# The first norm's gain: one row spread by TensorE in place of a broadcast load

## The reference, cut to what matters

```python
def rmsnorm(x, g, eps=NORM_EPS):
    xf = x.astype(jnp.float32)
    y = xf * lax.rsqrt(jnp.mean(xf * xf, axis=-1, keepdims=True) + eps)
    return (y * g.astype(jnp.float32)).astype(x.dtype)
...
        xn = rmsnorm(x, norm_mix_pre[l])
        q, k, v, u_a, v_a = project(xn, w_in[l])
```

## Time and profile before

| | |
|---|---|
| time before, median of 3 runs | 1381.57 us (1380.36 to 1382.99) |
| the profiled execution's own time | 1382.37 us |
| its span | 1380.6 us |
| PE busy in the span | 1357.9 us (98%) |
| DVE, ACT, POOL busy | 701.5, 461.0, 169.9 us |
| granted clock in the page's 40 slices | 9 in each |
| PE busy from 0 to 5 us, 5 to 10, 10 to 15, 15 to 20 | 0.00, 4.34, 3.71, 4.31 us |
| PE busy from 20 to 25, 25 to 30, 30 to 35 us | 5.00, 5.00, 4.88 us |

### The profile page before, as it was taken

How to read it: one execution, slowest core, us unless ns; L and a number is a source line. 1 busy time by engine, 2 the same in 40 slices (tenths; PEclk the granted TensorE clock), 3 DMA queues, 4 the chain that set the end, 5 groups by cost and what they waited for, 6 DMA issues and landing times.

```text
span 1380.6 us, 22412 instructions
## 1 busy us (share of the span) xinstructions
PE 1357.9 (98%) x8658; PEld 1220.7 (88%) x8658; DVE 701.5 (51%) x1173; ACT 461.0 (33%) x782; POOL 169.9 (12%) x323
## 2 busy tenths in 40 slices
PE   7999999999999999999999999999999999999998
PEld 6999999966657788899898989898989898999986
DVE  6233322176778564554546464636454545364556
ACT  6321021055667543343131313131323232222332
POOL 2253000022222221120000000000000000000003
PEclk9999999999999999999999999999999999999999
DMA  7202123266673623132020201111110202010116
GB/s 266 63 31 66 31 77 99 73 193 185 182 234 133 206 103 119 47 107 77 16 76 15 75 17 61 30 61 30 58 33 22 69 15 76 15 64 27 47 46 134
DMA packets 93577, 113.17 MB, mean 82 GB/s; under 512 B 6460, under 2 KB 65509, under 8 KB 93509
## 3 DMA queue, kind: packets, MB, share of 16 engines
q1 hardware_dynamic: 90377, 105.26, 24.2%
q0 software_dynamic: 992, 3.54, 1.5%
q10 hardware_dynamic: 2140, 3.46, 0.7%
HBM read 97.28 MB, written 14.69 MB: 81 GB/s over the span
## 4 chain that ended last, share of the span: by engine, by line
PE 93%; DVE 2%; issue 2%; ACT 1%; DMA 1%; POOL 0%; SPq 0%; POOLq 0%; DVEq 0%; ACTq 0%
PE PS L2361 37%; PE PS L2073 17%; PE PS L2425 16%; PE PS L2304 7%; PE PS L2166 2%; PE PS L2128 2%; PE PS L2189 2%; PE PS L2440 2%; PE PS L2455 2%; PE PS L2235 1%; PE PS L2212 1%; PE PS L2058 1%; DMA x_in<-in_x_prompt_dram 1%; PE PS L2296 1%; PE PS L2154 1%
## 5 line engine op out<-in xcount | busy, mean ns | idle before, releaser
L2361 PE MATMUL PS<-act_lo,wu_hi 128*128 128x364 f32 (+1 forms) x1056 | 346.4, 328 | 0.0
L2361 PE MATMUL PS<-act_hi,wu_hi 128*128 128x364 f32 (+1 forms) x1056 | 346.0, 328 | 0.2 <-DVE wu_lo L1850 0.2
L2361 PE MATMUL PS<-act_hi,wu_lo 128*128 128x364 f32 (+1 forms) x1056 | 346.0, 328 | 0.0
L2361 PEld LDWEIGHTS PS<-act_hi,wu_hi 128*128 128x128 f32 x1056 | 198.6, 188 | 1.0 <-DVE wu_lo L1850 0.5
L2361 PEld LDWEIGHTS PS<-act_lo,wu_hi 128*128 128x128 f32 x1056 | 198.2, 188 | 0.4
L2361 PEld LDWEIGHTS PS<-act_hi,wu_lo 128*128 128x128 f32 x1056 | 198.4, 188 | 0.0
L1836 DVE TENSOR_TENSOR y_acc<-y_acc,PS 128x512 f32<-128x512 f32 x162 | 111.1, 686 | 116.0 <-PE PS L2425 116.0
L2425 PE MATMUL PS<-wd_hi,g_hi 128*128 128x512 f32 x324 | 130.1, 401 | 0.0
L2425 PE MATMUL PS<-wd_lo,g_hi 128*128 128x512 f32 x324 | 127.9, 395 | 0.0
L2425 PE MATMUL PS<-wd_hi,g_lo 128*128 128x512 f32 x288 | 114.0, 396 | 0.0
L1230 ACT CAST g_hi<-conv 128x1088 fp32r<-128x1088 f32 x21 | 23.1, 1102 | 245.6 <-PE PS L2425 189.6
(11 more groups left out here) (280 smaller groups left out, 2382.7 us busy)
## 6 DMA issues: line engine op xcount, KB each, us to landing
wu_raw<-in_w_up_dram SPq DMA_DIRECT2D x44, 512.0 KB, 3.9
vpage<-in_cache_v_dram SPq DMA_DIRECT2D x64, 256.0 KB, 3.0
kpage<-in_cache_k_dram SPq DMA_DIRECT2D x60, 256.0 KB, 2.9
wd_raw<-in_w_down_dram SPq DMA_DIRECT2D x22, 512.0 KB, 5.3
w_raw<-in_w_in_dram SPq DMA_DIRECT2D x20, 512.0 KB, 4.7
x_in<-in_x_prompt_dram SPq DMA_DIRECT2D x8, 512.0 KB, 7.0
wo_raw<-in_w_out_dram SPq DMA_DIRECT2D x8, 512.0 KB, 5.6
x_res<-in_x_prompt_dram SPq DMA_DIRECT2D x8, 512.0 KB, 4.2
```

Source lines behind the costliest of these rows:

```text
L2361: mm = nc.tensor.matmul(PS[:, 3 * half + c, 0:kept(c)], a[:, half, k, :], b[:, k, KEPT[c]], start=(j == 0), stop=(j == len(parts) - 1))
```

## The change

The table's broadcast load behind tile 0 goes. In its place DVE zeroes `gain`, ACT's queue loads the 1024 values into its first row, and PE multiplies a 128x128 block of ones (`rel_rep` of head 3, before its own values are written) with it: two matmuls, 512 columns each, which leave the row in all 128 partitions of PSUM banks 2 and 3. Tiles 0 and 1 take the gain from there, and the later tiles from the table in SBUF, which SP now loads behind tile 2, once the two matmuls are done. The bias lines are spread differently over the streams. The rounding of the second weight piece on ACT moves ahead of the squares of tile 1.

```diff
--- before.py
+++ after.py
@@ -739,11 +739,12 @@
                 sp.wait_ge(nrm_ready, s - 2)
             sp.dma_start(x_in[0:rows(s), s % 3, :], x_tiles[s]).then_inc(x_loaded[s % 3], 16)
             if s == 0:
-                sp.dma_start(gain[:], norm_mix_pre[0:1, :].to_broadcast([P, D])).then_inc(gain_loaded, 16)
                 load_w(sp, 0)
             if s == 1:
                 load_w(sp, 1)
             if s == 2:
+                sp.wait_ge(line_ready, 1)
+                sp.dma_start(gain[:], norm_mix_pre[0:1, :].to_broadcast([P, D])).then_inc(gain_loaded, 16)
                 for i, lam in enumerate((lambda_q1, lambda_q2, lambda_k1, lambda_k2)):
                     sp.dma_start(lam_in[:, i, :], lam[0:1, :].to_broadcast([P, DH])).then_inc(setup_loaded, 16)
                 sp.dma_start(sub_gain[:], subln_gain[0:1, :].to_broadcast([P, DV])).then_inc(setup_loaded, 16)
@@ -930,6 +931,8 @@
         act.dma_start(rel_sb[:], rel_bias[:, :]).then_inc(line_loaded, 16)
         act.wait_ge(lines_zero, 1)
         act.dma_start(lines_sb[0:BUCKETS + 1, :], lines[:, :]).then_inc(line_loaded, 16)
+        act.wait_ge(rep_ready, 1)
+        act.dma_start(gain[0:1, :], norm_mix_pre[0:1, :]).then_inc(gain_loaded, 16)
         act.wait_ge(const_ready, 3)
         nc.scalar.activation(stat[:, 104:105], neg_half, ACT.Square)
         for s in range(STEPS):
@@ -943,7 +946,6 @@
             if s == 0:
                 act_split_w(act, 0, (0,))
                 xt_hi(0)
-            if s == 1:
                 act_split_w(act, 0, (1,))
             if s >= 3:
                 take_job(s - 3)
@@ -1432,11 +1434,15 @@
     def _(dve):
         def bias_tables():
 
+            nc.vector.memset(gain[:], 0.0).then_inc(rep_ready, 1)
             nc.vector.memset(rel_rep[:], 1.0).then_inc(rep_ready, 1)
             dve.wait_ge(line_loaded, 16 * 2)
-            dve.wait_ge(rep_ready, 1)
-            for h in range(H):
-                nc.vector.tensor_copy(rel_rep[0:BUCKETS, h, :], rel_sb[:, h:h + 1].to_broadcast([BUCKETS, P])).then_inc(rep_ready, 1)
+            dve.wait_ge(rep_ready, 2)
+            for h in range(H - 1):
+                rep_line(h)
+
+        def rep_line(h):
+            nc.vector.tensor_copy(rel_rep[0:BUCKETS, h, :], rel_sb[:, h:h + 1].to_broadcast([BUCKETS, P])).then_inc(rep_ready, 1)
 
         def lam_tables():
             dve.wait_ge(setup_loaded, 16 * 5)
@@ -1448,7 +1454,7 @@
 
         def take_line(h):
 
-            dve.wait_ge(line_ready, h + 1)
+            dve.wait_ge(line_ready, h + 2)
             nc.vector.tensor_scalar(line_out[:, h, :], PS[:, 4 + h, 0:LINE], -1.0, None, ALU.mult).then_inc(line_taken, 1)
 
         def xt_lo(s):
@@ -1459,29 +1465,31 @@
                                         act_hi[:, 4 * h:4 * h + 4, cols(s)].bitcast(F32),
                                         ALU.subtract).then_inc(xt_lo_ready, 1)
         bias_tables()
-        dve.wait_ge(gain_loaded, 16)
+        take_line(0)
         for s in range(STEPS):
             r = rows(s)
             dve.wait_ge(rstd_ready, s + 1)
+            gained = PS[:, 2:4, :].rearrange("p a b -> p (a b)") if s < 2 else gain
+            if s == 2:
+                dve.wait_ge(gain_loaded, 32)
             if s >= 2:
                 dve.wait_ge(xt_ready, 2 * (s - 1))
             if s == 0:
-                nc.vector.scalar_tensor_tensor(x_nrm[:, 0, 0:512], x_in[:, 0, 0:512], rstd[:, 0:1], gain[:, 0:512],
+                nc.vector.scalar_tensor_tensor(x_nrm[:, 0, 0:512], x_in[:, 0, 0:512], rstd[:, 0:1], gained[:, 0:512],
                                                ALU.mult, ALU.mult).then_inc(half_ready, 1)
             cs = slice(512 if s == 0 else 0, D)
             nc.vector.scalar_tensor_tensor(x_nrm[0:r, s % 2, cs], x_in[0:r, s % 3, cs], rstd[0:r, s:s + 1],
-                                           gain[0:r, cs], ALU.mult, ALU.mult).then_inc(nrm_ready, 1)
+                                           gained[0:r, cs], ALU.mult, ALU.mult).then_inc(nrm_ready, 1)
             if s >= 2:
                 xt_lo(s - 1)
             if s == 0:
-                take_line(0)
-                take_line(1)
+                rep_line(H - 1)
                 dve_split_w(dve, 0, (0,))
                 xt_lo(0)
                 dve_split_w(dve, 0, (1,))
-            if s == 1:
+                take_line(1)
+            if s == 2:
                 take_line(2)
-            if s == 2:
                 take_line(3)
                 lam_tables()
             if s == 8:
@@ -1768,7 +1776,7 @@
         take_rows(NB // 2 - 1)
         split_rest(2)
 
-        dve.wait_ge(gain_loaded, 48)
+        dve.wait_ge(gain_loaded, 64)
 
         def x2_lo(t):
             for h in range(2):
@@ -1944,7 +1952,7 @@
         last_wd(1)
         last_lo(2)
 
-        dve.wait_ge(gain_loaded, 64)
+        dve.wait_ge(gain_loaded, 80)
 
         def last_add(t, half):
             s, n = LAST_TILES[t], 2 * t + half
@@ -2031,7 +2039,7 @@
         def bias_lines(heads):
             pe.wait_ge(line_loaded, 16 * 2)
             for h in heads:
-                pe.wait_ge(rep_ready, h + 2)
+                pe.wait_ge(rep_ready, h + 3)
                 nc.tensor.matmul(PS[:, 4 + h, 0:LINE], rel_rep[:, h, :], lines_sb[:], start=True, stop=True).then_inc(line_ready, 1)
 
         def project(n):
@@ -2074,8 +2082,13 @@
             mm.then_inc(job_ready, 1)
 
 
+        pe.wait_ge(rep_ready, 2)
+        pe.wait_ge(gain_loaded, 16)
+        for half in range(2):
+            mm = nc.tensor.matmul(PS[:, 2 + half, :], rel_rep[:, H - 1, :], gain[:, 512 * half:512 * half + 512], start=True, stop=True)
+        mm.then_inc(line_ready, 1)
         pe.wait_ge(pad_zero, 2)
-        bias_lines((0, 1))
+        bias_lines((0,))
         for s in range(STEPS):
             for h in range(2):
                 j = 2 * s + h
@@ -2091,10 +2104,10 @@
                                              ident[0:rows(s), 0:rows(s)])
                 mm.then_inc(xt_ready, 1)
             if s == 0:
-                bias_lines((2,))
+                bias_lines((1,))
                 pe.wait_ge(xt_lo_ready, 1)
                 project(0)
-                bias_lines((3,))
+                bias_lines((2, 3))
             if s >= 2:
                 pe.wait_ge(xt_lo_ready, 2 * s)
                 project(s - 1)
```

## The result

The change makes the kernel slower: 1386.22 us (median of 8 runs, 1384.7 to 1386.98) against 1381.55 (8 runs, 1380.21 to 1386.42), ratio 1.0031 with a 95% interval of 1.0022 to 1.0040. The forecast was 1384.3, range 1382.7 to 1386.3. The profiled execution took 1386.07 us with a span of 1384.3, against 1382.37 and 1380.6: 3.7 us more.

A forecast was written before the change was run, and what follows sets the result against it. PE is the bound, through the start of project(1) at 18.95 us. The change's steps put it at 21.65, 2.7 us late: 1385.1 against the profiled 1382.37, 1384.3 as a median, range 1382.7 to 1386.3.

The forecast's parts named there:

- gain matmuls start (T): On PE, 0.15 us after the row lands: 5.55 us, between 4.25 and 6.15; later steps are counted from it.
- sum against the profiled execution: project(1) at 21.65 against 18.95 carries to the end: 2.7 us late, 1385.1 against 1382.37.
- What bounds it: PE's unbroken run starts with project(1) at 18.95 us; what this moves, the end moves.
- The row's load: ACT's queue issues the row at 2.0 us; it lands at 5.4, between 4.1 and 6.0.
- The fit of 2.0 us plus bytes: Transfer time as about 2.0 us plus bytes over 436 GB/s; the row would land at 4.0 us.
- The two matmuls: Gain matmuls on PE at the low clock level: 0.855 us a pass, two passes each, 3.42 us plus 0.13.
- The rival in which the low level lasts: PE's clock not risen by project(0): +4.0 to +5 us, 1385.6 to 1386.6; chance 0.27.
- The queue on DVE: Taking line 0 ahead of tile 0's norm makes it wait for gain and line; project(0) at 14.5, 3.3 us later.
- The second piece's split: ACT's earlier rounding starts the second half of project(0) at 16.25, 2.1 rather than 3.3 us late: 1.2 back.
- Hidden loads: On SP, the gain table lands long before DVE wants it at 18 us; tile 3, wanted near 20, is hidden too.
- main line: Gain matmuls start 5.15 to 6.05, clock level risen before the transposes: +2.3 to +3.2 us, 1383.9 to 1384.8; chance 0.50.

The follow-up runs named there:

- a3: Changed kernel with the row's load first on ACT's queue, gain not zeroed, gain matmuls over one partition: 1381.91 us, ratio 1.0000 to the kernel before.
- a5: Changed kernel with SP's loads behind tile 0 held until the row has landed: 1384.45 us, ratio 1.0019 to the kernel before.
- a1: Changed kernel with line 0 taken behind the norm of tile 0 on DVE: 1384.16 us, ratio 1.0019 to the kernel before.
- a2: Changed kernel with the rounding of the second weight piece put back behind the square of tile 1: 1387.32 us, ratio 1.0037 to the kernel before.
- b1: Kernel before with only the earlier rounding of the second weight piece, ahead of the square of tile 1: 1381.42 us, ratio 0.9996.
- b2: Kernel before with SP's load of tile 3 held until act_lo of tile 0 is made: 1381.54 us, ratio 0.9992.
- b4: Kernel before with the gate's twelve small loads moved behind tile 6: 1383.59 us, ratio 1.0014.
- b3: Kernel before with the earlier split of the second weight piece and the gate's small loads behind tile 6: 1382.82 us, ratio 1.0011.
- c2: Changed kernel with row first over one partition, line 0 taken later, gate's small loads behind tile 6: 1383.87 us, ratio 1.0016 to the kernel before.
- c3: Changed kernel with row first over one partition and line 0 taken behind the norm of tile 0: 1381.92 us, ratio 1.0003 to the kernel before.
- c1: Changed kernel with row first over one partition, 20 warming transposes on PE, line 0 taken later: 1381.78 us, ratio 0.9998 to the kernel before.
- a4: Changed kernel with 20 transposes of the identity on PE ahead of the gain matmuls: 1383.82 us, ratio 1.0010 to the kernel before.

## Why the prediction was right, and where it was off

| step | forecast | measured |
|---|---|---|
| gain matmuls start (T) | 5.55 | 6.72 |
| line 0 taken | T + 5.05 | T + 4.87 |
| first norm | 11.1 | 12.06 |
| `project(0)` | T + 8.94 | T + 8.65 |
| its second half | T + 10.7 | T + 10.38 |
| transposes of tile 1 | T + 13.5 | T + 13.18 |
| `project(1)` | T + 16.1 | T + 15.78 |
| tile 6 issued | 24.9 | 25.90 |
| sum against the profiled execution | +2.7 | +3.7 |

**What bounds it.** Right: the delay of `project(1)`, 3.55 us, went through to the end as 3.7. Beyond 22 us PE had the stop for tile 6 that was there before, and 0.24 us more ahead of `project(2)` (25.44 to 26.47, 1.03 us in place of 0.79).

**The row's load** is the term that was mis-sized. The step "so I take 5.4, near the upper row" bounded the landing by 6.0, from what `lines_sb` took. It landed at 6.59, so T was 6.72, outside the bounds of 4.25 to 6.15. What the runs showed in its place: it lands 2.3 to 2.4 us after issue with little around it (a3, a5) and 4.55 in the crowd. My bound took the neighbour on the same queue as the worst case. That neighbour had been issued 0.8 us earlier, which is the likely reason that it was quicker, though no run shows it. The trace of before also held small loads that took longer: `lam_in` (32 KB) 8.1 to 8.3 us and `sub_gain` (64 KB) 8.8, on SP's queue behind the large ones. The Trainium skill's rule of serving queues in turn, a packet at a time ("DMA: Bandwidth & Descriptors", "Queues, rings and completion order"), agrees in sign. No run here shows the packets' order on one engine. The fit of 2.0 us plus bytes that the prediction quotes stands in the Trainium skill ("DMA: Bandwidth & Descriptors", "Anatomy of one DMA") for DMAs that GpSimd issues. The row went out on ACT's queue, and the sum did not use the fit.

**The two matmuls** were right at 0.85 us a pass (the line behind them at T + 3.55). The level rose some 4.4 us after PE's first work, not 5.4 as in the trace of before, so line 0 was out 0.2 us sooner. The rival in which the low level lasts did not come.

**The queue on DVE** was right to 0.15 us from the taking of line 0 on, and a1 shows that one taking moved back is worth 0.6 to 1.0 us. The norm with its operand in PSUM takes 0.74 us for 512 columns, as from SBUF (0.75).

**The second piece's split** was right. By the prediction's own measure, the first half of `project(0)` came 4.17 us late and the second 2.92, so 1.25 us came back where 1.2 was forecast. a2 shows that 1.0 of it is the split's. In the kernel before it gives nothing that shows in the time (b1): the squares that it pushes back carry the norm of tile 2 and the loads behind.

**Hidden loads** were right: b2 for a hold of tile 3, and the table was there for the norm at 18.98 without a wait.

**The time.** The traces differ by 3.7 us where 2.7 was forecast: 1.17 more by the late row, 0.32 less by the steps from there to `project(1)`, and 0.15 more behind it. Of the medians' 4.7 us the pair of traces explains 3.7. The interval of the ratio, 3.0 to 5.5 us, holds both, and a difference of this size between executions is common here (below). The remaining 1.0 was not traced. Part of it can lie in the trace of before, whose opening is the latest of the three with its code (`project(1)` at 18.95, 18.39, 18.21), and part in the eight executions: the larger samples of the kernel before in the other runs have medians of 1381.66 to 1382.28.

The measured 1386.22 lies within the range by 0.08 us, and that is luck. The main line ended at 1384.8. The room above it was there for the rival in which the low level lasts (1385.6 to 1386.6), and that rival didn't come. A late row and the untraced 1.0 us filled it instead.

## What to carry to other kernels

A load that is replaced must first be shown to be waited for, and its replacement priced in place. The broadcast landed at 6.65 us and the norm could start at 7.07 (in b2 and b4 the norm waited for it last, at 6.79 and 6.70, so it was level with `rstd`); the row, four passes of PE at its lower level and a line taken ahead of the norm brought 12.06. A small load issued among large ones took 4.55 us here where it took 2.3 without them, so one that must be quick goes first. The opening of one and the same code differed by 0.7 us between three traces, so a forecast of a few microseconds is better read from more than one. And where a loading queue issued just in time (b3, b4, c2), moving loads from ahead of one tile to ahead of the next only moved the stop.

## What the runs showed of the hardware

- A 4 KB row took 4.55 us to land among 512 KB loads, 2.4 us when first in its queue, and 2.3 us from the same place with the others held.
- The lower level lasted some 3.6 us after PE's first work in a1 (the pair of passes at 10.21 took 0.91), 4.4 in the changed kernel and 5.4 in the kernel before. It lasted some 10.8 in a3 (starts 0.21 us apart to 14.08, with a stop of 1.3 us from 8.7 to 10.0), about 10 in c2 and c3, and some 12.7 in c1, where PE waited for nothing in that time. These four have passes over one partition. It cannot be read off the granted clock's column of those stretches, which reads 1.00, but from the distance of starts.
- Stops of 1.78, 1.57 and 1.90 us near 37 us were followed by 24 matmuls in 4.6 us in place of 3.1, at a granted clock of 0.50 (a4, b4, c2). After a stop of 1.81 us in b3 the clock stayed at 1.00 and the pace the same.
- Executions of one kernel differ in mean granted clock, and the time goes with it: of 26 executions of the kernel before beside a1 to a4, seven read 0.999 and took 1380.07 us in the median, eight read 0.996 and took 1383.38. There is one trace of each kernel, so where the clock falls is seen only across kernels. Windows of PE from 470 to 475 us, in the kernel before and in b1 (columns: stretch, its length, busy and count of PE, weight loads, DVE, ACT, POOL, granted clock, DMA share, GB/s):

```profile
470.00:475.00 5.00, 5.00 (x26) 4.18 (x26) 1.06 (x2) 1.63 (x3) 0.00 (x0) 0.70 0.67 253
```

```profile
470.00:475.00 5.00, 4.63 (x44) 4.00 (x48) 1.71 (x3) 1.93 (x5) 0.42 (x2) 1.00 0.76 258
```

In before, changed, a1, a5 and b2 the clock falls to between 0.66 and 0.75 in one such stretch from 470 to 480 us, and the mean clock is 0.997 to 0.998. In a2, a3, b1 and c3 it reads 1.00 there, and the mean is 0.999. From PE's taking up of tile 6 to the end the first five took 1345.9 to 1346.3 us, the other four 1344.1 to 1344.6. So 1.5 to 2 us of a difference between two single executions can come from there.
